# Moving one cast per pair of heads from VectorE to ScalarE in a two-block transformer kernel

## The reference, cut to what matters

```
def token_mixer(h, w_in, w_out, sinks, bias_hb):
    proj = h @ w_in
    ...
    s = einsum(q, k) * scale + bias ; masked ; p = softmax(s)     # per head, 256 x 256, causal
    out = einsum(p, v)                                            # per head, 256 x 64
    return jnp.concatenate([out_a, out_b], axis=-1) @ w_out       # 256 x 1024 @ 1024 x 1024
```

## Time and profile before

| | |
|---|---|
| median of 3 runs | 752.66 us (752.41 to 753.68) |
| profiled execution, its own time | 755.74 us |
| span of its trace, first to last instruction | 754.0 us |
| granted TensorE clock | 1.000 of full speed |
| busy: PE / DVE / ACT / POOL | 715.0 / 513.4 / 444.2 / 37.9 us |
| the eight splits of pairs start | 97.7 to 139.5 us |

### The profile page before, as it was taken

How to read it: one execution, slowest core, us unless ns; L and a number is a source line. 1 busy time by engine, 2 the same in 40 slices (tenths; PEclk the granted TensorE clock), 3 DMA queues, 4 the chain that set the end, 5 groups by cost and what they waited for, 6 DMA issues and landing times.

```text
span 754.0 us, 12098 instructions
## 1 busy us (share of the span) xinstructions
PE 715.0 (95%) x4126; PEld 611.1 (81%) x4126; DVE 513.4 (68%) x738; ACT 444.2 (59%) x696; POOL 37.9 (5%) x69
## 2 busy tenths in 40 slices
PE   0599999999999999999999999999999999999998
PEld 0488966699999888877989787778788888888886
DVE  6778689787877755456657575765667777777443
ACT  0554778666666644355456587565557777776331
POOL 4000000100000100014101000000000000000000
PEclk9999999999999999999999999999999999999999
DMA  8999887457787666635764654556346666666651
GB/s 307 349 326 367 255 244 276 139 181 218 221 244 266 207 222 195 195 113 138 220 187 127 223 177 129 175 161 195 113 140 175 190 191 176 188 193 196 197 193 56
DMA packets 137554, 152.07 MB, mean 202 GB/s; under 512 B 6189, under 2 KB 111784, under 8 KB 137516
## 3 DMA queue, kind: packets, MB, share of 16 engines
q1 hardware_dynamic: 135714, 146.86, 62.6%
q10 hardware_dynamic: 1804, 4.74, 1.8%
HBM read 150.14 MB, written 1.44 MB: 201 GB/s over the span
## 4 chain that ended last, share of the span: by engine, by line
PE 52%; DVE 2%; issue 0%; ACT 0%; DVEq 0%; ACTq 0%
PE acc L1460 11%; PE acc L1468 10%; PE acc L1470 9%; PE acc L1469 9%; PE acc L1461 6%; PE acc L1449 1%; PE acc L1448 1%; PE acc L1447 1%; PE aux L1436 1%; DVE wl L1002 0%; DVE x_rows L1071 0%; PE aux L1665 0%; ACT wh L614 0%; PE aux L1783 0%; PE aux L1857 0%
## 5 line engine op out<-in xcount | busy, mean ns | idle before, releaser
L1002 DVE TENSOR_TENSOR wl<-raw,wh 128x1024 fp32r<-128x1024 f32 x215 | 263.6, 1232 | 147.6 <-ACT wh L614 146.5
L614 ACT ACTIVATE wh<-raw 128x1024 fp32r<-128x1024 f32 x215 | 226.0, 1056 | 125.4 <-PE acc L1470 112.8
L1447 PE MATMUL acc<-xT,wh 128*128 128x256 f32 x440 | 125.1, 284 | 3.4 <-DVE xT L1044 2.2
L1460 PE MATMUL acc<-xT,wh 128*128 128x512 f32 x352 | 124.5, 399 | 0.3 <-DVE xT L1035 0.3
L1449 PE MATMUL acc<-xT,wl 128*128 128x256 f32 x440 | 124.5, 283 | 0.0
L1448 PE MATMUL acc<-xT,wh 128*128 128x256 f32 x440 | 124.5, 283 | 0.0
L1468 PE MATMUL acc<-wh,xT 128*128 128x512 f32 (+1 forms) x272 | 107.9, 397 | 0.3 <-issue 0.3
L1470 PE MATMUL acc<-wh,xT 128*128 128x512 f32 (+1 forms) x272 | 104.4, 384 | 0.0
L1469 PE MATMUL acc<-wl,xT 128*128 128x512 f32 (+1 forms) x272 | 104.3, 384 | 0.0
L1461 PE MATMUL acc<-xT,wl 128*128 128x256 f32 x352 | 98.9, 281 | 0.0
L1447 PEld LDWEIGHTS acc<-xT,wh 128*128 128x128 f32 x440 | 84.4, 192 | 5.5 <-DVE xT L1044 2.3
(11 more groups left out here) (278 smaller groups left out, 851.1 us busy)
## 6 DMA issues: line engine op xcount, KB each, us to landing
raw<-in_w_in SPq DMA_DIRECT2D x66, 512.0 KB, 3.7
raw<-in_w SPq DMA_DIRECT2D x64, 512.0 KB, 4.4
raw<-in_w_ffn_in SPq DMA_DIRECT2D x44, 512.0 KB, 4.3
raw<-in_w_ada SPq DMA_DIRECT2D x29, 512.0 KB, 6.8
raw<-in_w_ffn_out SPq DMA_DIRECT2D x22, 512.0 KB, 3.2
raw_more<-in_w_ada SPq DMA_DIRECT2D x11, 512.0 KB, 7.4
raw<-in_w_out SPq DMA_DIRECT2D x11, 512.0 KB, 3.3
rows_tmp<-in_w_ada ACTq DMA_DIRECT2D x8, 512.0 KB
```

Source lines behind the costliest of these rows:

```text
L614: A(wh[:, s, :], raw_unit, ACT.Copy).then_inc(rounded, 1)
L1002: V.tensor_tensor(wl[:, s, :], raw_slot(r), wh[:, s, :].bitcast(f32), ALU.subtract).then_inc(split_ready, 1)
L1447: mm(bank[:, 0:ROWS], wh[:, s, w], hi, start=(kt == 0), stop=False)
L1460: mm(bank[:, :], wh[:, s, w], moving[:, kt, :], start=(kt == 0), stop=False, skip_group_check=True)
```

## The change

ScalarE writes the high part of each pair's weighted values. The step `mix_pair_high(p)` stands in ACT's list at the end of slot i = 2p + 3, behind `scale_head(i)` (in slot 3 behind `leave_bank` and `copy_probsT` too; in slots 16 and 17 there is no head left to scale, so in slot 17 it stands behind the weight unit and ahead of `gain_rows`). It takes over the waits that DVE had. DVE waits for the new semaphore `mix_high` and does the subtraction alone.

```
+        mix_high = sem("mix_high")
...
+            def mix_pair_high(p):
+
+                act.wait_ge(pv_done, 2 * p + 2)
+                if p == 0:
+                    act.wait_ge(unit_done, U_OUT1)
+                A(xT[:, p, 0:ROWS], aux[3][:, 0:ROWS], ACT.Copy).then_inc(mix_high, 1)
...
                 if 1 <= i < OUT_SLOT:
                     copy_probsT(i - 1)
+                if i >= 3 and i % 2 == 1:
+                    mix_pair_high((i - 3) // 2)
...
                 if i >= 3 and i % 2 == 1:
                     p = (i - 3) // 2
-                    dve.wait_ge(pv_done, 2 * p + 2)
-                    if p == 0:
-                        dve.wait_ge(unit_done, U_OUT1)
-                    split(xT[:, p, :], aux[3][:, 0:ROWS], mix_ready)
+                    dve.wait_ge(mix_high, p + 1)
+                    V.tensor_tensor(xT[:, p, ROWS:], aux[3][:, 0:ROWS], xT[:, p, 0:ROWS].bitcast(f32), ALU.subtract).then_inc(mix_ready, 1)
```

## The result

The changed kernel takes 758.64 us (median of 6 runs, 758.21 to 760.32) against 753.17 us of the kernel before (6 runs, 752.41 to 754.22). The ratio is 1.0073, with a 95% interval of 1.0061 to 1.0086: slower by 0.73%, some 5.5 us. The profiled execution took 758.45 us with a span of 756.7 us, and in it the clock was granted in full. The forecast was 759.1 us.

What follows compares the result with a forecast made beforehand. DVE's instruction list was taken to bound the attention slots, ACT 0.06 us behind; 0.43 + 0.75 + 4 x 0.81 + 0.90 + 1.08 = 6.40 us on the 752.66 us median gives 759.1 us, range 757.4 to 760.8.

Steps and rivals of the forecast that it cites:

- slot 3: First pair: ACT's cast follows `copy_probsT`, so DVE's subtraction starts at 98.61 instead of 98.18, 0.43 us late.
- slots 5 and 6: Subtraction 0.91 us late in slot 5, less slot 6's old 0.16 us wait for ACT: 0.75 us.
- slots 7, 9, 11, 13: Subtraction 0.87 us late in each, less the even slot's old 0.06 us wait: 0.81 per pair, 3.24 us.
- slot 15: Subtraction at 134.54 instead of 133.64; PE already idles for what follows, so all 0.90 us reaches PE.
- slot 17: ACT's gain copies queue behind the cast, which waits for weighted values; PE's L1710 starts 1.08 us late.
- DVE's list is the bound, and ACT stands 0.06 us behind it: Attention slots: the 6.00 us period is the sum of DVE's instructions; even reciprocals wait 0.06 us for ACT.
- The high part comes too late, so that DVE waits: Odd slots 5 to 15: ACT casts only after scaling, so DVE waits some 1.2 us; reciprocals 6.8 us apart.
- The old small waits of even slots are taken back: Even slots: DVE arrives later than ACT's exponentials, so its waits of 0.06 us (0.16 in slot 6) vanish.
- Nothing gives it back: Behind the stage PE is full and its loads are ahead, so all later rows stay 6.4 us late; rival 2%.
- The clock did not fall: Rival: PE's added idle time drops the clock to 1.2 GHz in six periods, about 783 us; chance 3%.
- That help for a saturated DVE pays: Rival: ACT's casts in slots 5 to 15 shorten DVE's list, 2.1 us faster, 750.6 us; chance 2%.
- the case without the stall: Rival: PE's L1710 does not wait behind slot 17, so the sum is 5.3 us, time 758.0; chance 8%.

Runs made afterwards that it cites:

- d: Kernel before plus one extra ACT copy of 128x256 behind the scaling in slots 5, 7, ..., 15, splitting left on DVE; ratio 1.0009, stage +1.55 us.
- c: Changed kernel with the cast ahead of the scaling in slots 5 to 15 and the last cast behind the gain copies; ratio to kernel before 0.9991, stage +0.64 us.
- e: Kernel before, with DVE waiting for the odd head's scaling before its own copy in slots 5 to 15, no work moved; ratio 1.0092, stage +5.86 us.
- a: Changed kernel with only the last pair's cast put behind ACT's gain copies; ratio to kernel before 1.0061, stage +4.52 us.
- b: Kernel before with only the last pair cast by ACT, ahead of the gain copies; ratio 1.0014, stage +1.15 us.
- h: Kernel before with slots 5 to 13 casts on ACT ahead of `copy_probsT` and scaling, weight units of slots 6 to 12 moved; ratio 0.9977, stage -1.64 us.
- g: Kernel before with only weight units of slots 4 to 14 moved: ACT's part behind scaling, DVE's into the next slot; ratio 1.0029, stage +2.54 us.
- f: Kernel before with c's casts (ahead of scaling, last behind gain copies) and g's moved weight units together; ratio 1.0024, stage +0.60 us.

## Why the prediction was right

The forecast was 6.40 us on the median, 759.1 us. It is 5.5 us by the times, and 5.69 by the stage. That 758.64 us lies so near to 759.1 is in part luck: the median of the kernel before is 753.17 by six runs, 0.5 above the three that I built on, and this covers a part of what the sum has too much. Step by step, each shift taken from the rows of both traces against ACT's copy to `vall` in slot 3:

| term | forecast | measured |
|---|---|---|
| slot 3 | 0.43 | 0.24 |
| slots 5 and 6 | 0.75 | 0.64 |
| slots 7, 9, 11, 13 | 3.24 | 2.86 |
| slot 15 | 0.90 | 0.81 |
| slot 17 | 1.08 | 1.15 |
| sum | 6.40 | 5.70 |

- **DVE's list is the bound, and ACT stands 0.06 us behind it.** Shown by d (ACT's extra 0.3 us comes out in full) and c (DVE's saving is lost to ACT).
- **The high part comes too late, so that DVE waits.** Shown by e and c. In the change itself the period is 6.71 us (forecast 6.8) and DVE's wait 1.14 (forecast 1.2). The mis-sized part is the handing over from the cast to the subtraction. I took 0.10 us from another pair of rows and kept 0.03 as the bound; it is 0.03 to 0.04. The cast takes 0.36 us, and not 0.38. Together this is the 0.09 us by which each pair of slots 5 to 15 is too large. The Trainium skill's figure (VectorE: DVE Perf Modes, The TRN2 errata), which gave an estimate of 0.36 us for the cast, agrees with the new row.
- **Slot 3.** The subtraction is 0.36 us late and not 0.43, for the same reason. Here I missed something more: DVE's next row used to wait 0.12 us for PE's scores behind the split (98.64 against the 98.52 that its subtraction would have allowed), which covers a part of the delay.
- **The old small waits of even slots are taken back.** In the changed kernel the even reciprocal follows the ada step by 1.20 us, in slot 6 too.
- **ACT's queue behind slot 17.** Shown by a and b: 1.17 and 1.15 us for 1.08. This was given only from the order of the code, since the kernel before has no such wait.
- **Nothing gives it back.** I had written that I am wrong if the shift at 156 us is not that at the end. By the letter this came about: PE's first product of the next stage is 5.03 us later, and DVE's last row only 2.72. But the first of the 352 products of the second block is still 5.0 us later (571.4 against 566.4); what is lost behind that are the 2.3 us of those products. The six runs of each kernel, 5.5 us apart in their medians, say that the stage's loss is kept; a second trace of either kernel, which would show it directly, was not taken. The clock did not fall.
- **The rivals.** That help for a saturated DVE pays is wrong for this place and right in h. My price for it, 2.1 us, took off only the 0.06 to 0.16 us by which ACT held DVE up already, and not the cast's own 0.3 us on ACT, which comes out in the even slot: c, which has the cast nearly in time, gained nothing, and the weight unit had to move as well.
- **The range.** Its ends do not quite follow from their terms. The upper one is 752.66 + 7.4 + 1.0 = 761.1 us, where 760.8 is written, and the case without the stall reaches down to 752.66 + 5.9 - 1.08 - 0.25 = 757.2, where 757.4 is. The result lies inside either way.

## What to carry to other kernels

Work that is moved off the bounding engine must be finished before that engine gets there; if the helper can only start behind something that the bounding engine has just released, the move adds a round trip to its list. Look for the helper's idle time at the place where the work goes, since idle time elsewhere in the period hid nothing here (ACT had 0.9 us of it per period, and 0.3 us more work cost 0.3 us). And look at each engine's last turn by itself: a step that waits there for late data holds up whatever used to run past it.

## What was not expected of the hardware

The 352 products of 128x512 in the second block's gate and up stage take 391 ns on the mean in five of the profiles and 399 ns in the other five, with the granted clock shown as 1.00 there in all of them. This moves a whole execution by 2.3 us, over 40% of the effect that was looked for. What decides it is open: no kernel was profiled twice.

The clock can fall in this stage: in g it was half for some 3 us behind 2.60 us of idle time of PE, and in f, behind 2.52 us, it was not. The change made no such gap (PE's longest wait from 96 to 145 us is 1.6 us).

The time from the end of one ACT instruction to the start of the DVE instruction that waits for it was 0.03 to 0.04 us for the new cast (128x256) and its subtraction, but 0.10 us for the 128x512 pair and also 0.10 us in e, from ACT's L748 (113.47) to DVE's copy (113.57). Why is open too.
